# Expert GELU by its formula: cubic argument on DVE, tanh on ACT

## What is computed

```python
q = (xb @ w_pq).reshape(PEER_BLOCK, PEER_HEADS, 2, D_KEY // 2)
...
e = (jnp.take_along_axis(i1, ci // PEER_TOPK, -1) * N_KEYS
     + jnp.take_along_axis(i2, ci % PEER_TOPK, -1))
g = jax.nn.softmax(sc, axis=-1)
u = peer_u[e]
v = peer_v[e]
a = jax.nn.gelu(jnp.einsum('td,thkd->thk', xb, u).astype(jnp.float32))
return jnp.einsum('thk,thkd->td', (g * a).astype(v.dtype), v)
```

## Time and profile before

| | us |
|---|---|
| median of 3 runs | 1946.48 (1945.32 to 1952.69) |
| profiled execution | 1951.28 |
| its span, first to last instruction | 1949.5 |
| busy in it: PE, DVE, ACT, POOL | 1326.9, 1350.4, 793.6, 777.9 |
| DMA moved | 723.17 MB |

### The profile page before, as it was taken

One profiled execution on the slowest core, in us unless ns is written; L12 is line 12 of the kernel. 1 busy time (PEld: TensorE's weight loads), 2 busy tenths in 40 slices (PEclk: granted clock), 3 DMA queues, 4 the chain that ended last, 5 costly groups with the idle time before them and its releaser, 6 DMA issues.

```text
span 1949.5 us, 23865 instructions
## 1 busy us (share of the span) xinstructions
PE 1326.9 (68%) x7204; PEld 646.9 (33%) x7204; DVE 1350.4 (69%) x3212; ACT 793.6 (41%) x2757; POOL 777.9 (40%) x796
## 2 busy tenths in 40 slices
PE   7999886774764866656664655555746666677876
PEld 6765572331232333324321222122221333322221
DVE  6967898864748779888987753444444467886665
ACT  2132247772424344544543443333333223354554
POOL 0953324443434444455443333233233344444442
PEclk9999996776886677777776677766767555576977
DMA  7012689999999999999999999999999999999997
GB/s 299 1 44 93 200 312 421 397 373 421 411 387 415 352 421 421 421 421 420 417 391 416 421 414 420 420 421 421 422 412 422 421 420 405 412 416 417 413 422 287
DMA packets 101024, 723.17 MB, mean 371 GB/s; under 512 B 12016, under 2 KB 12784, under 8 KB 20784
## 3 DMA queue, kind: packets, MB, share of 16 engines
q0 software_dynamic: 82944, 604.02, 75.5%
q1 hardware_dynamic: 17968, 117.77, 15.4%
HBM read 714.78 MB, written 4.87 MB: 369 GB/s over the span
## 4 chain that ended last, share of the span: by engine, by line
DMA 37%; PE 22%; DVE 13%; ACT 7%; issue 6%; POOL 1%; POOLq 0%; ACTq 0%; DVEq 0%; another core or an unknown queue 0%
DMA R<-d_uv,W 37%; PE bank L1408 8%; DVE R L2169 7%; PE bank L1321 3%; PE bank L1295 3%; PE bank L1162 3%; ACT W L1682 1%; ACT L1679 1%; PE bank L1291 1%; PE bank L1154 1%; ACT W L1687 1%; PE bank L1355 1%; POOL R L919 1%; PE bank L1208 1%; ACT W L1650 1%
## 5 line engine op out<-in xcount | busy, mean ns | idle before, releaser
L919 POOL DMA_INDIRECT R<-d_uv,W x576 | 671.8, 1166 | 1011.1 <-PE bank L1408 832.0
L2169 DVE CUSTOM_DVE_ANT_0 R<-R,W 128x1024 f32<-128x1024 f32 x576 | 696.7, 1223 | 473.1 <-DMA R<-d_uv,W 456.1
L1408 PE MATMUL bank<-R,W 128*32 128x512 f32 x2296 | 473.4, 848 | 558.9 <-ACT W L1687 550.5
L1650 ACT CAST W<-W 128x2 uint32<-128x2 f32 x292 | 55.7, 192 | 883.5 <-DVE W L2169 866.8
L1408 PEld LDWEIGHTS bank<-R,W 128*32 128x32 f32 x2296 | 81.6, 125 | 798.5 <-ACT W L1687 724.6
L1687 ACT ACTIVATE W<-W 128x32 f32<-128x32 f32 x576 | 153.5, 313 | 9.7
L1682 ACT ACTIVATE W<-W 128x1 f32<-128x1 f32 x576 | 138.2, 287 | 9.7
L1321 PEld LDWEIGHTS bank<-E 128*128 128x128 f32 x864 | 123.7, 230 | 35.7 <-issue 35.7
L1321 PE MATMUL bank<-E 128*128 128x128 f32 (+1 forms) x864 | 129.7, 317 | 0.5 <-issue 0.5
L963 PE MATMUL bank<-E,W 128*128 128x256 f32 (+1 forms) x384 | 102.9, 427 | 10.1 <-DMA E<-d_xT 7.9
L963 PEld LDWEIGHTS bank<-E,W 128*128 128x128 f32 x384 | 75.4, 200 | 31.5 <-issue 10.1
(11 more groups left out here) (334 smaller groups left out, 1807.9 us busy)
## 6 DMA issues: line engine op xcount, KB each, us to landing
E<-d_kc SPq DMA_DIRECT2D x8, 2560.0 KB
E<-d_w_pq SPq DMA_DIRECT2D x6, 2048.0 KB, 12.7
E<-d_vc SPq DMA_DIRECT2D x8, 1536.0 KB, 26.2
R<-d_uv,W POOLq DMA_INDIRECT x576
E<-d_w_out SPq DMA_DIRECT2D x4, 2048.0 KB, 12.7
E<-d_vc SPq DMA_DIRECT2D x8, 1024.0 KB, 30.5
W<-d_w_in SPq DMA_DIRECT2D x3, 2048.0 KB, 21.1
W<-d_w_pq SPq DMA_DIRECT2D x3, 2048.0 KB, 8.2
```

What stands on the lines that cost most here:

```text
L919: pool.indirect_dma_start(ring[r], None, A["uv"], bass.IndirectOffsetOnAxis(ap=stage[:, half, s:s + 1], axis=0),).then_inc(landed[r], 16)
L1408: last = mm(acc(half, TG * column_group(js[s], half), TG), wsel[:, r, :], ring[r][:, D + half * 512:D + half * 512 + 512], start=False, st ...
L1650: return nc.scalar.copy(stage[:, half, PAIR * x:PAIR * x + PAIR], egall[:, 0, at])
L2169: last = nc.vector.tensor_tensor_reduce(ring[r][:, 0:D], ring[r][:, 0:D], hrep[:, js[s], :], 1.0, 0.0, ALU.mult, ALU.add, dots[:, x, s:s + 1])
```

## The change

The GELU of a pair is written out. DVE forms, directly behind the pair's dot products x, square = (sqrt(2/pi) 0.044715 x) x, half_x = (0.5 x) g with the softmax weight g out of `egall`, and arg = (square + sqrt(2/pi)) x. ACT takes the tanh of arg for both slots in one instruction, and the two weight instructions become Identity with half_x as scale and as bias: half_x tanh + half_x. New waits: DVE waits for its own dot products (`dotted`), for its own square (`shaped`), and at the head of `experts` for `laid`, since it now reads `egall`; ACT waits for `shaped` before the tanh. The other GELUs (the state-space part) stay as they are.

```diff
+        arg = view(Wf, 10112, 2, HALF)
+        half_x = view(Wf, 10120, 2, HALF)
+        square = view(Wf, 10128, 2, HALF)
...
                     act.wait_ge(dotted, n)
                     copy_stage(x, g, column(i, RING + x * HALF + g * PAIR, PAIR)).then_inc(staged, 1)
                     two = slice(g * PAIR, g * PAIR + PAIR)
-                    f(gel[:, x, two], dots[:, x, two], ACT.Gelu_apprx_tanh).then_inc(gelued, 1)
+                    act.wait_ge(shaped, 2 * n)
+                    f(gel[:, x, two], arg[:, x, two], ACT.Tanh).then_inc(gelued, 1)
                     act.wait_ge(gelued, n)
                     for s in range(g * PAIR, g * PAIR + PAIR):
-                        last = f(wts[:, x, s:s + 1], gel[:, x, s:s + 1], ACT.Copy,
-                                 scale=egall[:, 1, column(i, x * HALF + s, 1)])
+                        last = f(wts[:, x, s:s + 1], gel[:, x, s:s + 1], ACT.Identity,
+                                 scale=half_x[:, x, s:s + 1], bias=half_x[:, x, s:s + 1])
...
                 b = block_of(p0)
+                last = p1 * PAIR - 1
+                if last < QB * EXP:
+                    dve.wait_ge(laid, last // (2 * PK) + 1)
+                else:
+                    dve.wait_ge(laid, min(4 * BLOCKS, 4 * QB + (last - QB * EXP) // PK + 1))
...
                     last.then_inc(dotted, 1)
+                    n = 4 * i + (2 * x + g + 1)
+                    two = slice(g * PAIR, g * PAIR + PAIR)
+                    dve.wait_ge(dotted, n)
+                    stt(square[:, x, two], dots[:, x, two], GELU * CUBIC, dots[:, x, two], ALU.mult, ALU.mult).then_inc(
+                        shaped, 1)
+                    stt(half_x[:, x, two], dots[:, x, two], 0.5, egall[:, 1, column(i, x * HALF + g * PAIR, PAIR)],
+                        ALU.mult, ALU.mult)
+                    dve.wait_ge(shaped, 2 * n - 1)
+                    stt(arg[:, x, two], square[:, x, two], GELU, dots[:, x, two], ALU.add, ALU.mult).then_inc(shaped, 1)
```

More of the change, by code:

```diff
@@ L55 @@
 NEG = -3.0e38
+GELU = float(np.sqrt(2.0 / np.pi))
+CUBIC = 0.044715
 def column(i, at, n):
@@ L588, in build @@
             sem(n) for n in ("ht_full", "ht_ready", "gate_full", "gate_sig", "gate_used"))
-        cneg_set, ss_first, carried = sem("cneg_set"), sem("ss_first"), sem("carried")
-        alpha_set, asc_ready = sem("alpha_set"), sem("asc_ready")
+        ss_first, carried = sem("ss_first"), sem("carried")
+        alpha_set, shaped = sem("alpha_set"), sem("shaped")
         pq_full, pq_ready, s_full, s_ready, s_used = (
```

## The result

| | before | after |
|---|---|---|
| median, us | 1950.99 (20 executions, 1943.79 to 1955.68) | 1956.51 (20, 1950.46 to 1960.01) |
| profiled execution; its span | 1951.28; 1949.5 | 1959.51; 1957.7 |
| ratio after / before | | 1.0033, 95% interval 1.0022 to 1.0045 |

The changed kernel is slower by 0.33%, 6.4 us by the ratio; the two medians lie 5.5 us apart. Forecast was 6.0 us faster and 1940.5 us, with a range of 1932 to 1953: the sign is wrong, and the time lies outside the range. Of the 16.0 us between 1940.5 and 1956.5, 4.5 are the level (the three executions shown before the change have a median 4.5 us under that of all 20); the other 11.5 are the 6.0 us forecast as a gain and the 5.5 us measured as a loss.

What follows compares the result with a forecast made beforehand. The DMA, at 421 GB/s, was taken as the bound, with some 33 us winnable. Terms -6.3, -1.0, +1.0, +0.3 and zeros elsewhere gave -6.0 us: 1940.5 us for the median, range 1932 to 1953.

Steps and rivals of the forecast that it cites:

- The gain in front: 350 to 450 us: loads 18.0 less 7.2 and 4.5 added, so -6.3 us; 266 to 350 us: -1.0 us.
- The price of a load: ACT: each table load costs 1.283 us with no drain behind it, where the skill's rule gives 2.66 us.
- The loads behind the front: Later stretches: loads won set against 0.40 + 0.25 us added per pair, counted as 0.
- The first rival: In front, waits are PE's and not ACT's, so only additions stay: +1.3 to +3 us, 1948 to 1949; chance 0.22.
- DVE's 0.40 us per pair: The three added DVE operations take 0.40 us per pair, 115 us over 288 pairs; bounds 0.30 and 0.75.
- What hides it: DVE's idle time before dot products, 456.1 us of waits for landings, covers the added DVE time; 0 from 700 to 1000.
- The threshold in 700 to 1000: DVE's added time decides there only from 0.41 us per pair on, or 0.51 with the ring's lag.
- the rival: DVE becomes the bound in 700 to 1000 us: at 0.75 us per pair, +14.5 us in all, 1961; chance 0.08.
- the ring's lag: 700 to 1000 us: the ring absorbs about 6 us before the rate falls: 19.9 less 7.5 less some 6.
- The longer way round: ACT's tail starts about 0.25 us later per pair: 4.5 us in 350 to 450, hidden where the DMA is full.
- Identity with two pointers: ACT's weights as Identity instead of Copy: 0 difference, bounds -0.1 to +0.1 us for each of two per pair.
- the two signs: Forecast wrong if a pair's DVE addition passes 0.51 us, or if 350 to 450 does not speed up.

Runs made afterwards that it cites:

- tanh kernel: Kernel before with the expert GELU replaced by Tanh of the dot product, nothing added, loads 133 to 43; measured twice: 1940.27 and 1944.04 us.
- e4: Changed form for pairs 0 to 35, GELU form of the kernel before for the other 252; 1946.43 us, 0.9974 of before.
- e1: Kernel before with the expert GELU replaced by Tanh of the dot product, nothing added; 1940.27 us, 0.9939 of before.
- e9: The same kernel as e1, run again on another chip; 1944.04 us, 0.9956 of before.
- e2: Tanh kernel plus the change's three DVE operations per pair, results unused and not waited for by ACT; 1956.28 us, 1.0030 of before.
- e12: Kernel before with GELU and all table loads kept, plus the three DVE operations per pair, unused; 1964.00 us, 1.0071 of before.
- e10: As e2, but the operations work on earlier pairs' data, so none waits for DVE's own last result; 1947.83 us, 0.9989 of before.
- e11: As e2, with the three DVE operations twice per pair, some 0.75 us of DVE; 1975.37 us, 1.0122 of before.
- e7: As e2, with the three unused DVE operations only in pairs 132 to 287; 1950.00 us, 0.9999 of before.
- e8: Changed form everywhere except pairs 72 to 131, which keep the GELU form; 1955.07 us, 1.0033 of before.
- e3: As e2, but ACT waits for arg and takes its tanh; weights stay Copy with one scale; 1955.59 us, 1.0018 of before.
- e14: Tanh kernel with four more unused Tanh on ACT per pair, DVE untouched; 1944.25 us, 0.9966 of before.
- e13: Tanh kernel with two more unused Tanh on ACT per pair, DVE untouched; 1942.55 us, 0.9968 of before.
- e17: Tanh kernel with eight more unused Tanh on ACT per pair, DVE untouched; 1949.96 us, 1.0001 of before.

## Why the prediction was wrong

**The gain in front, -6.3 and -1.0: right as a sum, and in part by luck.** 350 to 450 went from 388 to 417 GB/s, and by the landings after took 7.4 us less than before over gathers 0 to 71, against 7.3 in the sum. But the sum had 18.0 us for the loads less 7.2 and 4.5 for what is added, and the runs have 7.7 for the loads, which is all there was to win, and about 1 for what is added: two terms were too large and cancelled. The loads of 266 to 350 us won nothing (gathers 0 to 35: -0.5 us in before against the tanh kernel), where the sum had 1.0. The price of a load was right too: by the Trainium skill's page (ScalarE: Activation LUTs, What ACT_TABLE_LOAD costs) the stretch would win its whole 7.8 us, which by the landings cannot be told from 7.3; the rows, with 1.30 us from a load's start to its ACTIVATE, still show no drain behind it. The loads behind the front were worth nothing by the landings, as the sum had it, and by the times (e4 against e1 and e9, 0.9974 against 0.995) up to 4 us. That later part is within what the measurement can tell. The first rival, a front that is not won, falls with this.

**DVE's 0.40 us per pair: right in size.** The trace of after has 0.39, three operations 0.07 and 0.12 us apart. The prediction took from the Trainium skill (VectorE: DVE Perf Modes, The DRAIN you can't avoid) that the next operation starts only once the pipe is empty; the same section adds that an operation that is not held starts earlier, and with that sentence the trace agrees. Half_x waits for nothing and starts 0.07 us behind an operation of 0.16 us; square starts 0.04 us after the end of the read that it waits for, and arg 0.03 us after the end of square, while half_x still runs.

**What hides it: wrong, and this is the step that failed.** The prediction took DVE's waits for landings as cover: 456.1 us in all, and 24.8 us against 24.0 in the dense stretch, "that fits, barely", so 0 for 700 to 1000, 0 for 600 to 700 and 0 for everything later. The three operations alone cost 15.6 us without the loads (e2) and 13.9 with them (e12), and 12 by the landings, of which 1.6 in gathers 72 to 107, 2.4 to 143, 4.1 to 287 and 3.1 behind; the sum had 1.0 us for all that lies behind the front. The error is in reading a wait as slack. DVE's waits are one link of a closed ring: a wait of DVE before one dot product does not pay for work behind the next. Where landed slots queue behind DVE, the added time delays all of them, and they come free later; a stretch under 421 GB/s is not made good, since no slice of before or after runs above 422. The runs show the dose (e10, e2, e11) and that it needs no instruction of ACT (e2, e12). The longer queue is measured in front and in the dense stretch (there from 2.4 us to 2.8 and 5.2 in the mean); that it is the cause also behind 1000 us, where the queue shows no dose and e7 still costs, is not shown, and neither is why e8 gets nothing back.

**The threshold in 700 to 1000 (0.41 to 0.51 us per pair): right as a size, wrong as a switch.** At 0.39 us, below it, the dense stretch already paid 4.1 us, just past the upper end of "0 to 4 us"; at 0.75 us the gathers from 683 to 1067 us paid 18.7, where the rival had 14.2 after the ring's lag and 20.2 without. Only 6.0 of 24.8 us of DVE's waits were left at 0.39, so 18.8 of 24 us were in fact taken from waits, and the other 5 are about what the ring paid. The ring's lag of 6 us was made with "a way round of some 6", which no row shows: in the trace of before 9.6 us pass in this stretch from a landing to POOL's next gather into that slot. With it the lag is 2.8 us (an estimate, 19.9 - 7.5 - 9.6) and the rival's price 17.4, near the 18.7.

**The longer way round, +0.25 us per pair: right in size, and too dear in front at 4.5 us.** e3 has it, e2 does not, and e3 is not the slower; 0.36 us on ACT's part of the way cost 3 us in all (e14). It was charged where the rate was back at 420 GB/s once the loads were gone.

**Identity with two pointers: at the edge of its bound.** The group of before, which is in none of the rows:

```profile
L1682 ACT ACTIVATE W<-W 128x1 f32<-128x1 f32 x576 | 138.2, 287 | 9.7
```

379 ns against 287 for Copy with one, +0.092 us each, where the sum had 0 and the bound was 0.1. It takes back 53 us of ACT's saved 115, and tanh no longer overlaps the CAST, so that ACT's busy time fell by 45.7 us and not by the 115 of the forecast's last part; what this costs in time is 2.9 us between e3 and after, with an interval from about 0 to 6.

**The chances.** That the change is within 0.5% (0.68) is what came; but by luck: the cases that made up that chance were the forecast and the front not won, both with DVE's time nearly free. The range ended at 1953 because DVE's shortfall was held to be all or nothing in one stretch. And neither of the two signs by which the forecast was to be known as wrong appeared: a pair's addition stayed under 0.51 us, and 350 to 450 did speed up. From 700 to 1000 DVE's wait was 6.0 us and the rate 415, between the forecast's 0 to 5 with 418 and the rival's "under 405".

## What to carry to other kernels

In a closed ring of slots behind a saturated DMA, idle time of an engine is not slack for that engine. In this kernel what was added to every turn cost 12 to 16% of its time on the engine that is nearly full somewhere (DVE, 88% in one stretch), and 3 to 5% on one that is not (ACT; e13's 7% is within the noise of that). For another kernel these are a first guess, and a run with unused operations on the engine in question, as e2, measures the price. Work that is taken off an engine in one stretch should be paid for in that stretch alone: the DVE form in the 36 pairs where ACT was the limit, and GELU behind them, is faster (0.9974) than either kernel. And the level of a forecast should come from more than three executions, or be told as a difference. Parts of a few microseconds in single stretches can't be read from one execution each.

## What the runs showed of the hardware

- A table load occupies ACT 1283 ns, and its ACTIVATE starts 1.30 us after the load did (408.89, 410.19); 90 fewer of them were worth 9 to 10 us of 1951. By the landings all of it came from gathers 36 to 71, which land from 366 to 469 us; the 14 loads between 266 and 350 us cost nothing.
- A small ACTIVATE (128x1) takes 287 ns with one pointer operand and 379 with two (before, after). Those of 128x2 without a wait between them start 0.10 us apart (e14), so eight more added 0.73 us and not 1.6 (e17).
- Three DVE operations of 128x2 take 0.39 us in all, with two waits on DVE's own results (after), and 0.22 us without them (e10); 0.07 us from start to start without a wait.
